# A hybrid decoder layer: shift and scale computed by column halves, one conditioning step split in two, and key pages multiplied in two instructions

## The reference, cut to what matters

```python
mod = (silu(c) @ w_ada + b_ada)                       # 2048 -> 6 * 2048
sh1, sc1, gt1, sh2, sc2, gt2 = split(mod, 6)
h = rmsnorm(x, g_pre_mix) * (1 + sc1) + sh1
proj = h @ w_in                                       # 2048 -> 6144 (+16 for the gate)
# 8 stick-breaking attention heads; each sample also reads 8 pages of 128 cached keys and values
# 4 gated linear attention heads with a state
x = x + gt1 * rmsnorm(concat(heads) @ w_out, g_post_mix)
h = rmsnorm(x, g_pre_ffn) * (1 + sc2) + sh2
x = x + gt2 * rmsnorm((silu(h @ w_gate) * (h @ w_up)) @ w_down, g_post_ffn)
```

## Time and profile before

| | |
|---|---|
| median of 3 runs | 1493.67 us (1493.54 to 1495.06) |
| the profiled execution's own time | 1496.05 us |
| its span, first to last instruction | 1494.3 us |
| TensorE busy | 1428.4 us, 96% |
| VectorE busy | 921.6 us, 62% |
| ScalarE busy | 665.5 us, 45% |
| mean granted TensorE clock | 0.983 |
| DMA moved | 396.82 MB, 266 GB/s on average |

### The profile page before, as it was taken

How to read it: one execution, slowest core, us unless ns; L and a number is a source line. 1 busy time by engine, 2 the same in 40 slices (tenths; PEclk the granted TensorE clock), 3 DMA queues, 4 the chain that set the end, 5 groups by cost and what they waited for, 6 DMA issues and landing times.

```text
span 1494.3 us, 29193 instructions
## 1 busy us (share of the span) xinstructions
PE 1428.4 (96%) x11238; PEld 1273.0 (85%) x11238; DVE 921.6 (62%) x1519; ACT 665.5 (45%) x1303; POOL 103.8 (7%) x200
## 2 busy tenths in 40 slices
PE   6779999998899999998999999999999999999997
PEld 2247787887667777796899999999999999999997
DVE  2243588995777666368756766567665675446444
ACT  1023477777656454345543434434344343334333
POOL 0000311113322210000000000000000000200000
PEclk9979999999899999999999999999999999999999
DMA  9999999999999979985755565555655555855552
GB/s 370 422 343 364 390 391 405 374 352 391 396 370 343 340 255 356 409 307 225 250 182 183 170 193 173 181 182 170 191 174 181 182 170 192 231 181 181 181 178 95
DMA packets 139330, 396.82 MB, mean 266 GB/s; under 512 B 13162, under 2 KB 17681, under 8 KB 126433
## 3 DMA queue, kind: packets, MB, share of 16 engines
q1 hardware_dynamic: 118018, 319.66, 61.3%
q0 software_dynamic: 21232, 76.10, 13.4%
HBM read 382.28 MB, written 11.34 MB: 263 GB/s over the span
## 4 chain that ended last, share of the span: by engine, by line
PE 83%; DMA 11%; DVE 2%; ACT 2%; issue 1%; POOLq 0%; SPq 0%; POOL 0%; DVEq 0%; ACTq 0%
PE ps L1981 24%; PE ps L1982 24%; PE ps L1983 24%; DMA ada_s<-in_w_ada 5%; PE ps L1915 4%; DMA v_page<-in_cache_v 3%; PE ps L2113 2%; DMA ada_r<-in_w_ada 1%; PE ps L2039 1%; DMA raw<-in_w_ffn_gate 1%; DMA k_page<-in_cache_k 1%; ACT k_page L803 1%; DMA k_page<-in_cache_v 1%; ACT w_hi L715 0%; PE ps L2141 0%
## 5 line engine op out<-in xcount | busy, mean ns | idle before, releaser
L1981 PE MATMUL ps<-h_hi,w_hi 128*128 128x264 f32 x2304 | 667.8, 290 | 11.0 <-DVE h_lo L1249 3.6
L1982 PE MATMUL ps<-h_lo,w_hi 128*128 128x264 f32 x2304 | 659.2, 286 | 0.0
L1983 PE MATMUL ps<-h_hi,w_lo 128*128 128x264 f32 x2304 | 658.6, 286 | 0.0
L1981 PEld LDWEIGHTS ps<-h_hi,w_hi 128*128 128x128 f32 x2304 | 438.9, 190 | 55.8 <-issue 34.9
L1806 DVE TENSOR_TENSOR w_lo<-raw,w_hi 128x1024 fp32r<-128x1024 f32 x254 | 307.2, 1214 | 273.1 <-ACT w_hi L1047 271.7
L1047 ACT ACTIVATE w_hi<-raw 128x1024 fp32r<-128x1024 f32 x264 | 278.5, 1059 | 408.2 <-PE ps L1983 384.4
L1982 PEld LDWEIGHTS ps<-h_lo,w_hi 128*128 128x128 f32 x2304 | 438.2, 190 | 0.5
L1983 PEld LDWEIGHTS ps<-h_hi,w_lo 128*128 128x128 f32 x2304 | 436.9, 190 | 0.0
L1261 DVE TENSOR_TENSOR w_lo<-raw,w_hi 128x1024 fp32r<-128x1024 f32 x138 | 168.7, 1223 | 145.9 <-ACT w_hi L715 145.5
L715 ACT ACTIVATE w_hi<-raw 128x1024 fp32r<-128x1024 f32 x128 | 135.1, 1056 | 172.5 <-PE ps L1983 155.1
L1982 PE MATMUL ps<-act_lo,w_hi 128*128 (+1 forms) x704 | 200.4, 285 | 0.0
(11 more groups left out here) (362 smaller groups left out, 1213.8 us busy)
## 6 DMA issues: line engine op xcount, KB each, us to landing
ada_r<-in_w_ada SPq DMA_DIRECT2D x64, 1024.0 KB, 9.1
raw<-in_w_in SPq DMA_DIRECT2D x96, 512.0 KB, 8.3
raw<-in_w_ffn_gate SPq DMA_DIRECT2D x88, 512.0 KB, 3.5
raw<-in_w_ffn_up SPq DMA_DIRECT2D x88, 512.0 KB, 4.4
raw<-in_w_ffn_down SPq DMA_DIRECT2D x88, 512.0 KB, 4.6
ada_s<-in_w_ada SPq DMA_DIRECT2D x32, 1024.0 KB, 13.7
k_page<-in_cache_k POOLq DMA_DIRECT2D x64, 512.0 KB, 8.0
v_page<-in_cache_v POOLq DMA_DIRECT2D x38, 512.0 KB, 8.4
```

Source lines behind the costliest of these rows:

```text
L1981: mm(out, w_hi, xh, start=first, stop=False)
L1982: mm(out, w_hi, xl, start=False, stop=False)
L1983: return mm(out, w_lo, xh, start=False, stop=last)
```

## The change

Three edits.

1. The first 32 conditioning steps make column halves: steps 0 to 15 give the first 1024 columns of shift and of scale, steps 16 to 31 the second 1024. Each piece is now two runs of 4 KB in a row. With the first half of h done, the first four units of groups 0 and 1 (those whose rows lie in it) are done as units 0 to 7 behind steps 18 to 28, their weights loaded between the pieces. Units 8 to 15 are the second halves of both groups, and their tiles are added to those copied out before (`evac_sum`, on VectorE). The other steps are set anew: steps 0 to 15 at slots 9 to 32.
2. Of the second shift, only the first eight steps are done at even slots 34 to 48; the other eight come at slots 97 to 105, with a turn of their own at slot 106, and the sixteen of the second scale come at slots 108 to 123 instead of 96 to 114.
3. For an even key page VectorE does one product of 128x1024 and one sum instruction, which waits for it.

GpSimd's first five key page loads go ahead of the masks, and the gate's work moves five slots back.

```diff
+        NG = 2
+        NSPLIT = NG * UPC // 2
+        NSET = NIN + NOUT + NG
+        def unit_of(u):
+            if u < 2 * NSPLIT:
+                half, i = divmod(u, NSPLIT)
+                g, j = divmod(i, UPC // 2)
+                return g, j + half * UPC // 2
+            return divmod(u, UPC)
...
-        A_SLOT = {n: 3 + 9 * n // 8 for n in range(16)}
-        A_SLOT.update({16 + k: 25 + 2 * k for k in range(16)})
-        A_SLOT.update({32 + k: s for k, s in enumerate(
-            (96, 97, 98, 100, 101, 102, 103, 104, 105, 106, 107, 108, 110, 111, 112, 114))})
+        A_SLOT = dict(enumerate((9, 10, 12, 13, 14, 15, 16, 17, 19, 20, 22, 24, 26, 28, 30, 32)))
+        A_SLOT.update({16 + k: 34 + 2 * k for k in range(8)})
+        A_SLOT.update(dict(zip(range(24, 32), (97, 98, 100, 101, 102, 103, 104, 105))))
+        A_SLOT.update({32 + k: 108 + k for k in range(16)})
...
-        TURN_AT = {20: 2, 55: 3, 115: 4}
+        TURN_AT = {33: 2, 55: 3, 106: 4, 124: 5}
...
+            W_BEHIND = {16: 0, 17: 1, 19: 2, 20: 3, 22: 4, 23: 5, 25: 6, 26: 7, 29: 8, 30: 9}
             for n in range(6, 2 * KC):
                 sp.wait_ge(ads_used, n - 5)
-                sp.dma_start(ADS[n % 6][:, :], ada_start(n)).then_inc(ads_in[n % 6], 16)
-            for u in range(4):
-                w_load(u)
+                ada_first_load(n)
+                if n in W_BEHIND:
+                    u = W_BEHIND[n]
+                    if u >= 4:
+                        sp.wait_ge(lo_ready, u - 3)
+                    w_load(u)
...
             mod_row(0)
+            for i in range(3):
+                hi(i)
+                h_high(i)
+            for u in range(3, 7):
+                hi(u)
+            act.wait_ge(ads_used, 14)
+            for m in range(MT):
+                evac(0, m)
+            hi(7)
+            for m in range(MT):
+                evac(1, m)
+            hi(8)
+            hi(9)
             mod_row(1)
-            hi(0)
-            for i in range(NH):
-                h_high(i)
-                if i < 3:
-                    hi(i + 1)
+            h_high(3)
+            hi(10)
+            h_high(4)
...
+            def evac_sum(e, m):
+                if m < 3:
+                    dve.wait_ge(bank_done, 3 * e + m + 1)
+                else:
+                    dve.wait_ge(unit_used, SET_END[e])
+                dve.wait_ge(bank_out, MT * NG)
+                dst = unit_dst(e - NG, m)
+                v.tensor_tensor(dst, dst, ps[:, m, 0:T], ALU.add).then_inc(bank_out, 1)
...
-                    for h in range(H):
-                        hs = slice(h * DH, (h + 1) * DH)
-                        ins = v.scalar_tensor_tensor(kp[:, hs], kp[:, hs], 1.0, QBC[:, b % 2, hs], ALU.mult, ALU.mult,
-                                                     accum_out=ZD[:, b, pg * H + h:pg * H + h + 1])
-                    ins.then_inc(k_even, 1)
+                    link(v.tensor_tensor(kp[:, :], kp[:, :], QBC[:, b % 2, :], ALU.mult))
+                    v.tensor_reduce(ZD[:, b, pg * H:pg * H + H], kp[:, :].rearrange("p (h d) -> p h d", h=H), op=ALU.add,
+                                    axis=AX.X).then_inc(k_even, 1)
...
+            UNIT_BEHIND = {18: 0, 19: 1, 20: 2, 22: 3, 23: 4, 25: 5, 26: 6, 28: 7}
+            for n in range(KC, 2 * KC):
+                ada_first(n)
+                if n == KC + 1:
+                    mod_turn(0)
+                if n in UNIT_BEHIND:
+                    unit(UNIT_BEHIND[n])
+            mod_turn(1)
```

More of the change, by code:

```diff
@@ L491, in _ @@
                 w_unit(wg_v, 0, u, W_FFN + u - 3)
+                if u < 3:
+                    ada_load((48, 49, 54)[u])
             for n in range(55, 59):
@@ L542, in _ @@
             g.tensor_copy(ident_b[:, :], ident[:, :]).then_inc(consts, 1)
[L544 to L555, removed]
             pool.wait_ge(misc_in, 64)
-            pool.wait_ge(ada_used, 13)
+            pool.wait_ge(ada_used, 5)
             def k_page(n):
@@ new lines, in prompt, with low, samples @@
+            def prompt(i):
+                for k in range(*HPC[i]):
+                    ins = v.tensor_scalar(F_LO[:, k, 0:TP], F_LO[:, k, 0:TP], scale_t[:, k, 0:1], MOD[:, k, 0:1], ALU.mult, ALU.add)
+                ins.then_inc(h32_ready, 1)
+            def low(i):
+                cs = slice(*HPC[i])
+                dve.wait_ge(hhi_ready, i + 1)
+                v.tensor_tensor(H_LO[:, cs, :], F_LO[:, cs, :], H_HI[:, cs, :].bitcast(F32), ALU.subtract).then_inc(h_ready, 1)
+            def samples(q):
+                cs = slice(KC // 2 * q, KC // 2 * (q + 1))
+                dve.wait_ge(mod_done, q + 1)
+                link(v.scalar_tensor_tensor(scale_t[:, cs, :], MOD[:, KC + cs.start:KC + cs.stop, :], 1.0,
+                                            vec1[:, NMOD + cs.start:NMOD + cs.stop].unsqueeze(2).to_broadcast([P, KC // 2, NC]),
+                                            ALU.add, ALU.mult))
+                link(v.tensor_tensor(F_LO[:, cs, TP:T], F_LO[:, cs, TP:T], scale_t[:, cs, 1:NC], ALU.mult))
+                v.tensor_tensor(F_LO[:, cs, TP:T], F_LO[:, cs, TP:T], MOD[:, cs, 1:NC], ALU.add)
@@ L1271, in _ @@
             mod_part(0)
-            dve.wait_ge(mod_done, 1)
-            scales(vec1[:, NMOD:NMOD + KC], KC)
-            mod_part(1)
-            dve.wait_ge(mod_done, 2)
-            build_h(0)
+            samples(0)
+            for i in range(3):
+                prompt(i)
+                lo(i)
+                low(i)
+            for u in range(3, 10):
+                lo(u)
+            mod_part(1)
+            samples(1)
+            prompt(3)
+            low(3)
+            prompt(4)
+            lo(10)
+            low(4)
+            def evac_sum(e, m):
+                if m < 3:
+                    dve.wait_ge(bank_done, 3 * e + m + 1)
+                else:
+                    dve.wait_ge(unit_used, SET_END[e])
+                dve.wait_ge(bank_out, MT * NG)
+                dst = unit_dst(e - NG, m)
+                v.tensor_tensor(dst, dst, ps[:, m, 0:T], ALU.add).then_inc(bank_out, 1)
             def gate(h):
@@ L1684, in slot @@
                     fold(SQD[:, 12:16, :], MT, acc_ready)
+                if NG <= SET_AT.get(st, 0) < 2 * NG:
+                    for m in range(3):
+                        evac_sum(SET_AT[st], m)
             def gate_scales(gain, part):
@@ L1703, in fold @@
                 ins.then_inc(done, 1)
-            for st in range(NSLOT):
+            for st in range(NSPLIT, NSLOT):
                 slot(st)
@@ L1992, in unit @@
                     pe.wait_ge(mix_ready, j + 1)
-                first, last = j == 0, j == UPC - 1
+                first, last = set_of(u - 1) != e, u in SET_AT
                 for m in range(MT):
-                    if first and g > 0:
-                        pe.wait_ge(bank_out, MT * (g - 1) + m + 1)
+                    if first and e > 0:
+                        pe.wait_ge(bank_out, MT * (e - 1) + m + 1)
                     for kk in range(2):
```

279 lines of the change are left out of this document (145 added, 134 removed).

## The result

The changed kernel takes 1507.8 us (median of 4, 1503.7 to 1508.2) against 1494.4 (median of 4, 1493.5 to 1497.2): ratio 1.0073, 95% interval 1.0051 to 1.0095. It is slower; the forecast was 1493.5 and its range ended at 1502.5.

The account below looks back on a forecast made before the run. TensorE was taken to bound most of the kernel, with loads, VectorE and DMA limiting some stages. A 10.2 us lead less 9.0 given back, about 1 us laid aside, netted about 0: 1493.5 us, range 1486.5 to 1502.5.

Parts of the forecast that it names:

- The start: Up to unit 8: eight early units fit where TensorE waits for pieces; gives 5.2 us, bounds 0 and 9.
- the stall of unit 4: First stage: unit 4 waits for banks behind weight 6, starts at about 89.9 us; last step ends at 109.9.
- the low clock at unit 8: At unit 8, after a 6.8 us chain without units: the low clock again costs 2.5 to 2.9 us.
- the lead at slot 19: Unit 19 done at 173.7 us instead of 187.2, 13.5 us sooner, partly borrowed from steps moved behind slot 96.
- nothing on the path: Slots 11 to 16: eight `evac_sum` replace ScalarE copies while VectorE is half idle, at no cost to the path.
- the sentence on VectorE's gaps in part 3: Slots 20 to 50: gaps shrink from 9.5 to 2 us, VectorE needs 140.2 us, 5.4 more; VectorE costs 3.3.
- If its gaps don't close: Slower rival, slots 20 to 50: the 19 even pages cost all 12.9 us, 7.5 worse, 1501 us; chance 0.20.
- TensorE alone would have kept 13.5 less two more steps in these slots, 11.4: Slots 20 to 50: without VectorE's lateness 11.4 us of the 13.5 us lead would remain at slot 51.
- Slots 56 to 95: Stage that DMA bounds: later even pages cost 0 on the path, up to 4 us; page waits relieved 0, at most 4.
- The late steps: Behind slot 96: eight more steps at 1.04 us, 8.3, plus 0.7 for the seventh turn, give back 9.0 us.
- The rival of loads that don't fit: Slower rival, slots 108 to 123: at 359 GB/s each slot takes 4.4 instead of 3.97 us, 1500 us; chance 0.08.
- The sum: Whole span: 10.2 less 9.0 is 1.2 us faster, about 1 us laid aside, net about 0; median 1493.5 us.

Follow-up runs that it names:

- changed, half pages: The changed kernel with only half of each key page loaded, VectorE's products at full length from the query row alone; 1494.6 us, ratio 0.9995.
- experiment 9: The changed kernel with even pages as before (no sum instruction) and half of each key page loaded; 1486.6 us, ratio 0.9944.
- second profile: Profile of the unmodified changed kernel from its second set of runs, taken to stand for the usual run; span 1505.6 us.
- experiment 11: The changed kernel with matmuls of 14 of the 16 steps of slots 108 to 123 cut to 128 of 512 columns, loads whole; 1504.2 us, ratio 1.0061.

## Why the prediction was wrong

*The start* was right in its mechanism (the loads behind, the stall of unit 4, the low clock at unit 8) and 2 to 4 us short. The last step ended at 111.2 and 112.6 us for 109.9, unit 8 started at 117.5 and 118.9 for 116.8. What the sum left out is the clock behind the stall of unit 4: 0.55 granted over 3.8 us is 1.7 us. And the lead at slot 19 was 11.4 and 9.6 for 13.5, since after unit 8 TensorE waits twice more, 1.6 us for `q_rows` and 0.8 for an `evac_sum`, which the prediction had as "nothing on the path".

*The step that failed* is the sentence on VectorE's gaps in part 3: "gaps of 9.5 us, most of them waits for TensorE that vanish when it is late. If 2 remain: 125.3 + 12.9 + 2 = 140.2 us". 6.8 remained in the change and 7.1 in the sum instruction alone, where slots 20 to 50 took 9.2 us longer. The waits for the high part, which come from TensorE, did nearly vanish; the others did not, and they were nearly half of the gaps. The earlier trace rows had been misread: one of its eight waits for `w_hi`, 3.1 us long, ends where slot 20 begins and is no gap of these slots (VectorE's timeline before):

```profile
188.36 1.23 DVE L1261 TENSOR_TENSOR w_lo<-raw,w_hi 128x1024 fp32r<-128x1024 f32 x1 [3.12 <-ACT w_hi L715]
```

VectorE's gaps inside slots 20 to 50, summed from the timelines by what ended them, in us:

| gaps of VectorE | before | sum instruction alone | changed | changed, half pages |
|---|---|---|---|---|
| high part (ScalarE, after TensorE) | 5.1 | 0.6 | 1.3 | 1.3 |
| key page (DMA) | 2.4 | 3.7 | 2.9 | 0 |
| `kgs_rows` from ScalarE | 1.3 | 1.6 | 1.4 | 1.4 |
| the rest, pauses too short for the view of the waits | 0.7 | 1.2 | 1.2 | 1.2 |
| all | 9.5 | 7.1 | 6.8 | 3.9 |

So 4.4 us of the 9.5 did not depend on TensorE, and they grew to 6.5 and 5.5. GpSimd issues a key page only when an earlier one has been used up, so a part of the longer page waits may follow from VectorE's own lateness; how much was not measured. VectorE's lateness reaches TensorE through ScalarE's program and the tile copies, as shown at unit 32, and through the tree. The price and place were among the rivals ("If its gaps don't close", decided from 4 us left, chance 0.20); that rival took all 9.5 us as lasting, and 7.1 and 6.8 did. The sum instruction costs 7.6 us alone and 6.1 in the change; 3.3 were in the sum. In the change a part of it hides behind late pages: by slot 55 it is 2.4 and 5.5 us in the two profiles, of which 1.8 of the 5.5 are the later start.

*The second failed step* is "TensorE alone would have kept 13.5 less two more steps in these slots, 11.4". Without the sum instruction 5.1 us are left of the lead at slot 51 with part 2, and -2.3 without it; with half pages it is 11.4 (experiment 9). The earlier trace rows show a DMA share of 1.02 in slots 20 to 31; I named two engines near their limit there and it was three. No term of the sum priced the loads of 1 MB that part 1 adds to slots 20 to 50 (seven, two with part 2), nor that the key pages land later among them, and no rival had it. The half pages measured it: 7 us of slots 20 to 50, both for part 1 alone (145.6 against 138.7) and for parts 1 and 2 (142.0 against 135.1).

*Slots 56 to 95* were taken at 0 and were neutral within 1 us. TensorE waits 13.5 us for value pages from 343.6 to 530 us, against 11.2 (11.9 in the second profile), and the lead did not change by it.

*The late steps* were mis-sized: 9.0 forecast, 11.2 measured. From slot 107 on there are ten more steps, 11.9 us at 1.19 each. Two fewer stand between slots 96 and 106, and these gave back 0.7 us only: unit 97 takes 5.1 us with a step ahead of it and 5.0 without, and unit 107 4.1 and 3.4. The slot was forecast at 3.97 us and measured at 4.12, since a step costs 1.19 us and not 1.04. The rival of loads that don't fit (4.4 us a slot) was wrong as a time, though experiment 11 shows that DMA stands right behind TensorE (3.88 us a slot).

*The sum*: 13.5 - 3.3 + 0 - 9.0 = 1.2 us faster, against 9.6 - 11.3 + 0.4 - 11.3 = 12.6 slower in the second profile; of these 1.3 are given back after unit 125; why was not looked into.

The Trainium skill, "VectorE: DVE Perf Modes", section "The perf-mode tier table", has `tensor_reduce` at one element a cycle; the measured 1220 ns against 1217 for the product of the same 1024 elements (groups of the page) agree with it.

## What to carry to other kernels

Before the gaps of a nearly full engine are filled on paper, sort them by what ended them, inside the stretch alone. Here only the waits for TensorE, which VectorE itself holds up, shrank when it got later (5.1 to 0.6 us); those for key pages, for ScalarE's rows and the short pauses grew (4.4 to 6.5). Before a lead is booked, add up the bytes that must land behind it: where the DMA share was already 1.02, loads moved later took 7 us of it back. A step's price is the difference between two slots with and without it (1.19 us), not the busy time of its instructions (1.04).

## What the runs showed of the hardware

A reduction of 128x1024 fp32 into 128x8 takes as long as the two-source product of that shape (1220 and 1217 ns). Eight one-pass instructions of 128x128, product and sum in one, follow each other at 0.21 us and do a page in 1.70 us, where two long instructions need 2.39: fewer instructions were slower; each element passes VectorE twice there, once in each of the two instructions of 1.22 us. The matmuls of a step cut to a quarter of their columns still left 0.6 us of its 1.19 (slots of 3.5 against 2.93 us).
